# Attention scores of two layers as three rounded products instead of one full-precision product, and one more wait for GpSimd in block 1

## The reference, cut to what matters

```python
proj = jnp.einsum('bsd,dc->bsc', u, w_in[l])
(dq, dk, dv, rq, rk, rv, rg, gq, gk, gv, gate_logits) = split_cols(proj, IN_SPLITS)
# differential attention: 4 heads, each with two maps of head size 64
s = jnp.einsum('bqhmd,bkhmd->bhmqk', qb, k).astype(jnp.float32) * scale
# retention: 4 heads of key size 128, scores times a decay
# grouped-query attention: 8 query heads on 2 key heads of size 64
s = jnp.einsum('bqgrd,bkgd->bgrqk', qb, k).astype(jnp.float32) * scale
...
branches = jnp.stack([a, r, c], axis=2)
projected = jnp.einsum('bsnw,nwd->bsnd', branches, w_branch[l])
merged = jnp.sum(gates * projected, axis=2)
h = h + jnp.einsum('bsd,de->bse', merged, w_out[l])
```

## Time and profile before

| | |
|---|---|
| median of 3 runs | 2940.39 us (2938.97 to 2942.61) |
| the profiled execution | 2939.37 us, its span 2937.6 us |
| PE busy | 2889.7 us (98%), 14295 matmul records |
| DVE busy | 1834.2 us (62%) |
| ACT busy | 1413.2 us (48%) |
| GpSimd busy | 309.2 us (11%) |
| DMA engines | about 30% |

### The profile page before, as it was taken

The page is one execution under the profiler, slowest core; times in us unless marked ns, Lnnn a source line. Parts: engine busy times, 40 slices in busy tenths (PEclk is TensorE's granted clock), DMA queues, the critical chain, the costliest instruction groups (busy, mean ns, idle before and its releaser), DMA issues. The chain is left out here.

```text
span 2937.6 us, 38352 instructions
## 1 busy us (share of the span) xinstructions
PE 2889.7 (98%) x14295; PEld 2333.4 (79%) x14295; DVE 1834.2 (62%) x2319; ACT 1413.2 (48%) x2078; POOL 309.2 (11%) x210
## 2 busy tenths in 40 slices
PE   9999999999999999999999999999999999999999
PEld 7787778888788877677777889897667777888888
DVE  4437768345854667656644787867755744587784
ACT  3556425234533446645543654445654554464442
POOL 5002300000100002211112000001221111000000
PEclk9999999999999999999999999999999999999999
DMA  7322223333323332123322433323222322433322
GB/s 193 92 72 71 60 58 94 100 94 100 107 86 104 93 98 68 48 79 87 93 72 86 124 99 101 101 82 91 56 60 72 109 72 79 122 101 101 101 87 72
DMA packets 407184, 263.44 MB, mean 90 GB/s; under 512 B 29674, under 2 KB 396124, under 8 KB 407008
## 3 DMA queue, kind: packets, MB, share of 16 engines
q1 hardware_dynamic: 401072, 250.09, 29.3%
q0 software_dynamic: 5936, 11.03, 1.3%
HBM read 253.70 MB, written 5.64 MB: 88 GB/s over the span
## 5 line engine op out<-in xcount | busy, mean ns | idle before, releaser
L751 DVE TENSOR_TENSOR wL<-wR,wH 128x1024 fp32r<-128x1024 f32 (+2 forms) x261 | 314.6, 1205 | 303.8 <-ACT wH L746 278.4
L826 PE MATMUL ps<-uH,wH 128*128 128x512 f32 x1184 | 483.7, 409 | 1.9 <-ACT wH L746 1.7
L826 PE MATMUL ps<-uL,wH 128*128 128x512 f32 x1184 | 463.5, 391 | 0.0
L746 ACT ACTIVATE wH<-wR 128x1024 fp32r<-128x1024 f32 (+3 forms) x352 | 361.6, 1027 | 182.1 <-DMA wR<-in_ffn_w_down_dram 54.5
L784 POOL TENSOR_TENSOR wL<-wR,wH 128x1024 fp32r<-128x1024 f32 (+1 forms) x91 | 224.7, 2470 | 1647.5 <-ACT wH L746 1647.5
L826 PE MATMUL ps<-uH,wL 128*128 128x512 f32 x1184 | 305.3, 400 | 0.0
L826 PEld LDWEIGHTS ps<-uH,wH 128*128 128x128 f32 x1184 | 223.0, 188 | 70.6 <-issue 23.3
L826 PEld LDWEIGHTS ps<-uH,wL 128*128 128x128 f32 x1184 | 219.7, 189 | 54.7 <-issue 8.9
L826 PEld LDWEIGHTS ps<-uL,wH 128*128 128x128 f32 x1184 | 223.2, 189 | 50.1 <-issue 6.5
L813 PE MATMUL ps<-uH,wH 128*128 128x512 f32 x528 | 208.3, 394 | 2.2 <-ACT wH L746 2.2
L813 PE MATMUL ps<-uL,wH 128*128 128x512 f32 x528 | 205.5, 389 | 0.0
(11 more groups left out here) (590 smaller groups left out, 6385.3 us busy)
## 6 DMA issues: line engine op xcount, KB each, us to landing
wR<-in_w_in_dram SPq DMA_DIRECT2D x182, 512.0 KB, 3.8
wR<-in_ffn_w_up_dram SPq DMA_DIRECT2D x44, 512.0 KB, 3.8
wR<-in_w_mlp_in_dram SPq DMA_DIRECT2D x22, 512.0 KB, 3.7
dn0R<-in_w_mlp_out_dram SPq DMA_DIRECT2D x22, 512.0 KB
dn1R<-in_w_mlp_out_dram SPq DMA_DIRECT2D x22, 512.0 KB, 3.4
dn2R<-in_w_mlp_out_dram SPq DMA_DIRECT2D x20, 512.0 KB, 3.4
wR<-in_w_branch_dram SPq DMA_DIRECT2D x16, 512.0 KB, 3.4
wR<-in_w_out_dram SPq DMA_DIRECT2D x16, 512.0 KB, 3.9
```

Source lines behind the costliest of these rows:

```text
L746: st.f(st.e.activation(wH[:, slot, 0:n], wR[:, slot, 0:n], ACT.Copy), hi_ready, c + 1)
L751: st.f(st.e.tensor_tensor(wL[:, slot, 0:n], wR[:, slot, 0:n], wH[:, slot, 0:n].bitcast(F32), ALU.subtract), lo_ready, c + 1 if done is Non ...
L826: ins = pe.matmul(o[:, :], w[:, k, :], x[:, k, :], start=s == 0, stop=s == 3 * KD - 1)
```

## The change: what it does

The scores of all three mixers become three products of rounded parts, as the projections are. Each of the 21 rotated tiles of a layer is split once: ACT copies it into an fp32r tile `qkH` (`split_high`, counted in `score_high`), DVE subtracts (`split_low`, counted in `score_low`). PE's first score of a head now waits for `score_low` instead of `rope_done`. The splits stand at fixed places in ACT's and DVE's queues. A pair of scores is now six matmuls (three steps on two halves of the rows, 512 columns each) instead of four f32 ones of 256 columns, a retention score three instead of one. In block 1 GpSimd waits, after its last product, for DVE's three low parts.

```diff
 def weights_pool(e):
     for g in range(3):
         e.tensor_tensor(lT[:, g, :], lT[:, g, :], lx[:, 1, :], ALU.mult).then_inc(sem("alpha_ready"), 1)
+    e.wait_ge(sem("alpha_parts"), 3)
...
+    def split_high(st, kind, t, l):
+        e = st.e
+        e.wait_ge(sem("rope_done"), rope_base(kind, l)[0] + TILES[kind].index(t) + 1)
+        st.w()
+        st.f(e.activation(qkH[kind, t][:, :], qk[kind][:, t, :], ACT.Copy), score_high, split_nth(kind, t, l))
+    def split_low(st, kind, t, l):
+        e = st.e
+        e.wait_ge(score_high, split_nth(kind, t, l))
+        st.w()
+        st.f(e.tensor_tensor(qkL[kind][:, t, :], qk[kind][:, t, :], qkH[kind, t][:, :].bitcast(F32), ALU.subtract),
+             score_low, split_nth(kind, t, l))
...
-    def scores_pair(pe, groups, q, k):
+    def scores_pair(pe, groups, kind, q, n, k):
         outs = [g.open(pe) for g in groups]
-        for x in range(2):
+        cols = slice(n * P, (n + 1) * P)
+        parts = ((qkH[kind, q][:, cols], qkH[kind, k][:, :]), (qkH[kind, q][:, cols], qkL[kind][:, k, :]),
+                 (qkL[kind][:, q, cols], qkH[kind, k][:, :]))
+        for x, (a, b) in enumerate(parts):
             for m in range(2):
-                rows, keys = slice(HD * m, HD * m + HD), slice(256 * x, 256 * x + 256)
-                ins = pe.matmul(outs[m][:, keys], q[rows, :], k[rows, keys], start=True, stop=True)
-                if x == 1:
+                rows = slice(HD * m, HD * m + HD)
+                ins = pe.matmul(outs[m][:, :], a[rows, :], b[rows, :], start=x == 0, stop=x == 2)
+                if x == 2:
                     groups[m].close(ins)
...
 gqa_pe:   if n == 0:
-                pe.wait_ge(sem("rope_done"), b + 2 + p)
+                pe.wait_ge(score_low, split_nth("g", p if p else 4, l))
 gqa_act:
+                if u in (1, 4, 8):
+                    split_high(st, "g", (1, 4, 8).index(u) + 1, l)
...
+            if u == 17:
+                split_high(st, "d", 0, l)
+                split_high(st, "d", 4, l)
 gqa_dve:      follow("gs", u)
+                if u in (2, 5, 9):
+                    split_low(st, "g", (2, 5, 9).index(u) + 1, l)
+            if u == 18:
+                split_low(st, "d", 0, l)
+                split_low(st, "d", 4, l)
 diff_pe:  if n == 0:
-                pe.wait_ge(sem("rope_done"), b + 2 * h + 2)
+                pe.wait_ge(score_low, split_nth("d", 4 + h, l))
 diff_act:     follow("s", u)
+                if u in (1, 5, 9):
+                    h = u // 4 + 1
+                    e.wait_ge(misc_ready, M("gpv", 3, l=l).nth if u == 1 else M("s", 4 * h - 5, 1, l=l).nth)
+                    split_high(st, "d", h, l)
+                    split_high(st, "d", 4 + h, l)
 diff_dve:     follow("s", u)
+                if u in (2, 6, 10):
+                    split_low(st, "d", u // 4 + 1, l)
+                    split_low(st, "d", 5 + u // 4, l)
 ret_pe:
             if j == 0:
-                pe.wait_ge(sem("rope_done"), b + 2 * h + 2)
+                pe.wait_ge(score_low, split_nth("r", 4 + h, l))
             g = M("rs", h, j, l=l)
             o = g.open(pe)
-            g.close(pe.matmul(o[:, :], qk["r"][:, 4 + h, j * P:(j + 1) * P], qk["r"][:, h, :], start=True, stop=True))
+            cols, qH, qL = slice(j * P, (j + 1) * P), qkH["r", h], qkL["r"][:, h, :]
+            kH, kL = qkH["r", 4 + h][:, cols], qkL["r"][:, 4 + h, cols]
+            pe.matmul(o[:, :], kH, qH[:, :], start=True, stop=False)
+            pe.matmul(o[:, :], kH, qL, start=False, stop=False)
+            g.close(pe.matmul(o[:, :], kL, qH[:, :], start=False, stop=True))
 ret_act:
+        split_high(st, "r", 0, l)
+        split_high(st, "r", 4, l)
         decays(0)
         for h in range(4):
             if h < 3:
+                if h:
+                    e.wait_ge(misc_ready, M("rs", h - 1, 3, l=l).nth)
+                split_high(st, "r", h + 1, l)
+                split_high(st, "r", 5 + h, l)
                 decays(h + 1)
 ret_dve:
+        split_low(st, "r", 0, l)
+        split_low(st, "r", 4, l)
         exponents(0)
         for h in range(4):
             if h < 3:
+                split_low(st, "r", h + 1, l)
+                split_low(st, "r", 5 + h, l)
                 exponents(h + 1)
```

More of the change, by code:

```diff
@@ L2805, in build, with split_nth @@
     rsq = nrmt
+    qkL = {"g": kb("qkL_g", [P, 5, S], 92, F32R), "d": kb("qkL_d", [P, 8, S], 64, F32R), "r": kb("qkL_r", [P, 8, S], 16, F32R)}
+    HIGH_AT = {("g", 0): 46, ("g", 4): 102, ("g", 1): 106, ("g", 2): 108, ("g", 3): 110}
+    for h in range(4):
+        HIGH_AT["d", h], HIGH_AT["d", 4 + h] = (102, 104) if h % 2 else (106, 46)
+        HIGH_AT["r", h], HIGH_AT["r", 4 + h] = (78, 108) if h % 2 else (62, 70)
+    qkH = {x: kb(f"qkH_{x[0]}{x[1]}", [P, S], o, F32R) for x, o in HIGH_AT.items()}
+    SPLITS = [("g", t) for t in TILES["g"]] + [(kind, t) for kind in "dr" for t in TILES[kind]]
+    score_high, score_low = sem("cv0_ready"), sem("cv_ready")
+    def split_nth(kind, t, l):
+        return 12 + len(SPLITS) * l + SPLITS.index((kind, t)) + 1
+    def split_high(st, kind, t, l):
[9 more added lines that the diff above has]
+             score_low, split_nth(kind, t, l))
     def rope_base(kind, l):
@@ L3012, in rope_act @@
                 high(st, (kind, t), l)
+            if kind == "g" and x in (2, 3):
+                split_high(st, kind, order[x - 2], l)
             yield
@@ L3062, in rope_dve @@
                 low(st, (kind, t), l)
+            elif x == 4:
+                split_low(st, kind, order[0], l)
+                split_low(st, kind, order[1], l)
             if x > 0:
@@ L3127, in turn @@
         g.close(ins)
-    def scores_pair(pe, groups, q, k):
+    def scores_pair(pe, groups, kind, q, n, k):
         outs = [g.open(pe) for g in groups]
-        for x in range(2):
+        cols = slice(n * P, (n + 1) * P)
+        parts = ((qkH[kind, q][:, cols], qkH[kind, k][:, :]), (qkH[kind, q][:, cols], qkL[kind][:, k, :]),
+                 (qkL[kind][:, q, cols], qkH[kind, k][:, :]))
+        for x, (a, b) in enumerate(parts):
             for m in range(2):
-                rows, keys = slice(HD * m, HD * m + HD), slice(256 * x, 256 * x + 256)
-                ins = pe.matmul(outs[m][:, keys], q[rows, :], k[rows, keys], start=True, stop=True)
-                if x == 1:
+                rows = slice(HD * m, HD * m + HD)
+                ins = pe.matmul(outs[m][:, :], a[rows, :], b[rows, :], start=x == 0, stop=x == 2)
+                if x == 2:
                     groups[m].close(ins)
     def gqa_pe(pe, l, fill):
-        b, _ = rope_base("g", l)
         def score(u):
@@ L3144, in score @@
             if n == 0:
-                pe.wait_ge(sem("rope_done"), b + 2 + p)
-            scores_pair(pe, [M("gs", u, m, l=l) for m in range(2)], qk["g"][:, p, n * P:(n + 1) * P], qk["g"][:, 4, :])
+                pe.wait_ge(score_low, split_nth("g", p if p else 4, l))
+            scores_pair(pe, [M("gs", u, m, l=l) for m in range(2)], "g", p, n, 4)
         def turned(v):
@@ L3236, in gqa_dve @@
                 follow("gs", u)
+                if u in (2, 5, 9):
[3 more added lines that the diff above has]
+                split_low(st, "d", 4, l)
     def diff_pe(pe, l, fill):
-        b, _ = rope_base("d", l)
         def score(u):
@@ L3243, in score @@
             if n == 0:
-                pe.wait_ge(sem("rope_done"), b + 2 * h + 2)
-            scores_pair(pe, [M("s", u, m, l=l) for m in range(2)], qk["d"][:, h, n * P:(n + 1) * P], qk["d"][:, 4 + h, :])
+                pe.wait_ge(score_low, split_nth("d", 4 + h, l))
+            scores_pair(pe, [M("s", u, m, l=l) for m in range(2)], "d", h, n, 4 + h)
         def turned(v):
@@ L3403, in ret_pe @@
     def ret_pe(pe, l, fill):
-        b, _ = rope_base("r", l)
         def score(h, j):
             if j == 0:
-                pe.wait_ge(sem("rope_done"), b + 2 * h + 2)
+                pe.wait_ge(score_low, split_nth("r", 4 + h, l))
             g = M("rs", h, j, l=l)
             o = g.open(pe)
-            g.close(pe.matmul(o[:, :], qk["r"][:, 4 + h, j * P:(j + 1) * P], qk["r"][:, h, :], start=True, stop=True))
+            cols, qH, qL = slice(j * P, (j + 1) * P), qkH["r", h], qkL["r"][:, h, :]
[3 more added lines that the diff above has]
+            g.close(pe.matmul(o[:, :], kL, qH[:, :], start=False, stop=True))
         def value(h):
```

## The result

| | before | after |
|---|---|---|
| median (four runs each) | 2940.68 us (2938.97 to 2942.61) | 2965.22 us (2962.55 to 2965.81) |
| the profiled execution, its span | 2939.37, 2937.6 us | 2962.55, 2960.7 us |
| ratio of the medians, 95% interval | | 1.0081 [1.0068, 1.0095] |

Slower by 0.8%.

The account below looks back on a forecast made before the run. PE, busy 98% of the span and running its queue in order, was taken to bound the kernel. +10.6 us a layer, +21.2 for two, less 1.0 in block 1, gave about +20: 2960 us, range 2948 to 2970.

Parts of the forecast that it names:

- The largest term: First retention score: PE waits for DVE's low part of key tile 4, +11.9 us a layer.
- Rival 1: First retention score: no wait, low parts ready in time; without 11.9 + 2.3 us a layer 2932 us; chance 0.06.
- The clock: Behind the retention wait: PE restarts at the 1.2 GHz level, 8 to 14 slower matmuls, +2.3 us a layer.
- The start of the differential stage: PE waits behind ACT's two copies, +1.4 us, and for DVE's two subtractions, +1.2 us, in each layer.
- The products: Scores in three products: 0.18 us saved a pair, 28 pairs kept, 0.17 us a retention product; -7.7 us a layer.
- rivals 2 and 3: Score pairs: entry and exit costs go away, 2938 us (chance 0.05); or the halves don't overlap, 2999 us (chance 0.04).
- Block 1: GpSimd's subtraction moves behind DVE's low parts, so PE's products come earlier: -1.0 us, bounds 0 and -1.6 us.
- its sign: Changed profile, block 1: L1701 about 1.4 us earlier against its neighbours.
- what the splits cost where they are covered: Most splits hide behind PE's full queue; only DVE's after grouped-query blocks 2 and 5 cost, +1.5 us a layer.

Follow-up runs that it names:

- e_ret_early: Changed kernel with the first retention head's splits moved from the start of the retention queues into the differential stage; 2940.48 us, ratio to the kernel before 1.0000.
- e_fourpass: Changed kernel, all splits and waits kept, but each score one four-pass f32 product of the high parts alone; 2979.08 us, ratio to the kernel before 1.0131.
- e_rope_x3: Changed kernel with DVE's two subtractions for the first grouped-query tiles one step earlier, ahead of clearing a tile; 2960.37 us, ratio to the kernel before 1.0066.
- e_diff_early: Changed kernel with e_ret_early's move and the first differential head's splits moved earlier in the grouped-query stage; 2936.8 us, ratio to the kernel before 0.9985.
- e_block1: Kernel before with only GpSimd's wait in block 1 for DVE's three low parts added; 2939.03 us against 2940.81, ratio 0.9995.

## Why the prediction held, and the step that failed

**The largest term was right.** The wait of 11.9 us measured 11.67 at the matmul and 11.8 in the sum. It was read from one row of the kernel before and the order of `ret_dve`, and e_ret_early shows that it and what follows from it are as large as the whole slowdown. Rival 1 (no such wait) is what that experiment builds; it forecast 2932 us, and came to 2940.5. The rival left out that the later heads' splits lose their cover once PE does not stand (2.5 and 2.2 us at the first value product), and it shares with the sum the term that failed (2.1 us a layer, below). The prediction had said that they cost nothing because DVE and ACT catch up during the wait; that was right for the kernel as changed, and the condition mattered.

**The clock.** 2.3 us were priced with 11 or 12 matmuls at 0.20 us extra; it was thirteen, 2.7 us. The step behind the same wait of 11.7 us lost between 1.8 and 2.7 us in the six stages of the changed kernel, e_fourpass and e_rope_x3, so the term has a scatter of its own of about 1 us a layer.

**The start of the differential stage.** 1.4 and 1.2 us were forecast; PE's waits are 1.3 and 1.0, the stretch 2.4 us against 2.4, and e_diff_early takes exactly that away.

**The products.** A pair at 1.09 us was right to the hundredth, so rivals 2 and 3 fall: entry and exit costs stay, and the halves overlap. A retention product saves 0.23 instead of 0.17 us. The 0.86 us of before was taken from one place, less two intervals of 0.23; over a whole step of 16 filling matmuls and a product (4.53 us before, 4.31 after) the difference is 0.22. Of the grouped-query pairs six tenths of the saving were kept, 0.10 us each, where three quarters were forecast. These misses nearly cancel, and that is luck: 8.1 against 7.7 us.

**Block 1** gained 1.95 us on the spot, more than the bound of 1.6 us: 1.4 us at the first product, as its sign said, and 0.5 us at the two behind it, which wait for the other low parts. At the start of the layer 1.2 us were left in the profiled execution, against 1.0 forecast; with the scatter of 2.3 us seen in e_block1 that nearness is luck.

**The step that failed** is "what the splits cost where they are covered", and in it the words "most are behind PE's full queue". The 1.5 us that it had, on DVE's subtractions after blocks 2 and 5, were right: e_fourpass has 1.6 us, at those two places. What it left at nothing, without a line, is the price of the first head's two subtractions inside `rope_dve`: 2.1 us a layer. The gap before them looked like cover, 1.68 us idle with 1.5 us to fill it; it was in use, though not by DVE. GpSimd's subtraction ran in it, and the two DVE subtractions, both inputs in SBUF, did not get on beside that. The trace of before had the warning: L3031, which reads PSUM, kept its 0.69 us at 1140.29 beside GpSimd, while L3038 behind it, on two SBUF tiles, took 1.93. Block 1's low parts were read as such a collision in the same prediction, and not applied here. The account closes: from the gap to the first maxima, DVE's instructions took 3.3 us longer beside GpSimd than alone in the kernel before, 5.5 us in the changed one and 4.5 us in e_rope_x3, and PE's step lost 2.1 us in the changed kernel and 1.1 us in e_rope_x3.

The Trainium skill states this in "SBUF — State Buffer", Who interferes with whom: a DVE instruction with two SBUF inputs contends with a GpSimd instruction that reads SBUF, over ports whose lock is exclusive. The trace agrees: 1.49 us become 3.66, by 2.17, beside a GpSimd instruction of 2.35 us, and L3064 with its PSUM input at 1138.77 keeps 0.69 us inside GpSimd's 1138.34 to 1143.73.

In the grouped-query stage the miss is 2.8 us a layer: 2.1 for the first head's subtractions, 0.5 for savings swallowed beyond those forecast, 0.1 for the covered splits. The clock (0.4) and the retention products (0.8 the other way) leave 2.4, 4.9 us for both layers. Block 1 and the stretches outside the layers gave 1.8 us more than forecast. By the traces that is 23.3 against 20.2 us. The rest of the 5 us is scatter between executions: the profiled one lies 2.7 us under its own median, and that of before 1.3. What the slower ones lost was not profiled.

## What to carry to other kernels

A result that is computed in good time but converted in an in-order queue is available when that queue comes to the conversion; look for the instruction that stands ahead of it, not at the engine's busy share. Moving two copies and two subtractions earlier in their queues was worth 24.7 us here, while the products for which the change was made gave 14 to 16 us. After a long wait is removed, look at once at what it had been covering. And before an instruction on two SBUF tiles is put into a gap on DVE, look at GpSimd's row for the same time: in this gap 1.49 us of work became 3.66.

## What was not expected of the hardware

- Two DVE subtractions of 128x512 with both inputs in SBUF take 1.49 us alone and 3.66 us beside a GpSimd subtraction that began 0.03 us earlier. A DVE instruction with one input in PSUM keeps its 0.69 us in the same company.
- A retention product of 128x512: 0.226 us less in three one-pass steps than in the four-pass form, a pair on 64 rows 0.175 us less; the cost of going to 64 rows and back, 0.09 and 0.11 us, is the same for both forms.
- After a wait of 11.7 us PE made thirteen matmuls at the 1.2 GHz level, 2.7 us more than at 2.4 GHz.
- Two waits of PE of about 2.2 and 1.8 us, 20 us apart, were followed by the 1.2 GHz level in two of ten grouped-query stages and by no change of clock in the other eight, with the same instructions. It costs 2.2 us a stage: a scatter that looks like noise in the medians and has a place in the trace.
